# Gates of expert tiles 32 to 127 by adding DMAs into a table in HBM, in place of one-hot products, in a two-layer PEER kernel

## The reference

```python
q = (xt @ w_q).reshape(n_tok, 8, 2, 128)
s = einsum('thpc,hpkc->thpk', q, sub_keys)
sv, si = top_k(s, 16)
cand = sv[:, :, 0, :, None] + sv[:, :, 1, None, :]
cand_idx = si[:, :, 0, :, None] * 128 + si[:, :, 1, None, :]
best, pos = top_k(cand.reshape(n_tok, 8, 256), 16)
eidx = take_along_axis(cand_idx, pos)
g = softmax(best)
act = gelu(einsum('ted,td->te', u_tab[eidx], x))
out = einsum('te,ted->td', g * act, v_tab[eidx])
```

## Time and profile before

| | us |
|---|---|
| median of 3 runs (lowest, highest) | 2098.67 (2096.07, 2100.24) |
| the profiled execution | 2098.75 |
| its span, first to last instruction | 2096.9 |

### The profile page before, as it was taken

How to read it: one execution, slowest core, us unless ns; L and a number is a source line. 1 busy time by engine, 2 the same in 40 slices (tenths; PEclk the granted TensorE clock), 3 DMA queues, 4 the chain that set the end, 5 groups by cost and what they waited for, 6 DMA issues and landing times.

```text
span 2096.9 us, 40394 instructions
## 1 busy us (share of the span) xinstructions
PE 2055.7 (98%) x16458; PEld 1889.3 (90%) x16458; DVE 1635.7 (78%) x3068; ACT 960.7 (46%) x1642; POOL 339.8 (16%) x245
## 2 busy tenths in 40 slices
PE   8999999999999999999999999999999999999998
PEld 7899999999889988887897999999998899888886
DVE  7887995555887688978799779965557777789776
ACT  5654553344433343445655545533334433444443
POOL 0014000000000064642110050000000000456420
PEclk9999999999999999999999999999999999999999
DMA  5354554444554457897322435544445544567873
GB/s 180 111 156 130 178 158 157 154 154 157 171 171 147 145 163 233 293 316 230 125 90 65 145 123 163 170 156 154 148 157 172 171 147 147 163 228 259 301 245 103
DMA packets 112935, 358.34 MB, mean 171 GB/s; under 512 B 17264, under 2 KB 27760, under 8 KB 112496
## 3 DMA queue, kind: packets, MB, share of 16 engines
q1 hardware_dynamic: 99888, 319.99, 47.2%
q0 software_dynamic: 12288, 33.60, 4.9%
q10 hardware_dynamic: 576, 2.18, 0.3%
HBM read 349.09 MB, written 6.63 MB: 170 GB/s over the span
## 4 chain that ended last, share of the span: by engine, by line
PE 84%; DVE 12%; ACT 2%; issue 2%; DMA 1%; SPq 0%; DVEq 0%; ACTq 0%
PE ps L878 15%; PE ps L879 14%; PE ps L880 14%; PE ps L909 11%; PE ps L910 10%; PE ps L911 10%; PE ps L956 6%; DVE w_lo L1470 2%; DVE work L1356 2%; DMA land<-stream_dram 1%; ACT w_hi L583 1%; PE ps L1037 1%; DVE hidden L1356 1%; DVE work L1364 0%; DVE hidden L1376 0%
## 5 line engine op out<-in xcount | busy, mean ns | idle before, releaser
L1470 DVE TENSOR_TENSOR w_lo<-land,w_hi 128x1024 fp32r<-128x1024 f32 x562 | 684.8, 1219 | 275.3 <-ACT w_hi L583 274.7
L583 ACT CAST w_hi<-land 128x1024 fp32r<-128x1024 f32 x592 | 621.2, 1049 | 441.1 <-PE ps L911 351.0
L878 PE MATMUL ps<-act_hi,w_hi 128*128 128x288 f32 x2688 | 809.2, 301 | 12.8 <-DVE act_lo L1196 5.9
L879 PE MATMUL ps<-act_hi,w_lo 128*128 128x288 f32 x2688 | 794.9, 296 | 0.0
L880 PE MATMUL ps<-act_lo,w_hi 128*128 128x288 f32 x2688 | 791.9, 295 | 0.0
L878 PEld LDWEIGHTS ps<-act_hi,w_hi 128*128 128x128 f32 x2688 | 505.4, 188 | 18.4 <-issue 10.9
L880 PEld LDWEIGHTS ps<-act_lo,w_hi 128*128 128x128 f32 x2688 | 507.7, 189 | 0.0
L879 PEld LDWEIGHTS ps<-act_hi,w_lo 128*128 128x128 f32 x2688 | 506.7, 188 | 1.0
L909 PE MATMUL ps<-w_hi,g_hi 128*128 128x512 f32 x1024 | 404.9, 395 | 3.6 <-DVE g_lo L1745 3.6
L910 PE MATMUL ps<-w_lo,g_hi 128*128 128x512 f32 x1024 | 399.1, 390 | 0.0
L911 PE MATMUL ps<-w_hi,g_lo 128*128 128x512 f32 x1024 | 398.8, 389 | 0.0
(11 more groups left out here) (214 smaller groups left out, 1353.8 us busy)
## 6 DMA issues: line engine op xcount, KB each, us to landing
land<-stream_dram SPq DMA_DIRECT2D x592, 512.0 KB
act_d<-smp_stage SPq DMA_DIRECT2D x64, 64.0 KB, 3.3
hidden<-stream_dram,smp_idx POOLq DMA_INDIRECT x128, 5.5
x<-x_dram SPq DMA_DIRECT2D x4, 288.0 KB, 6.8
y_t_dram<-hidden SPq DMA_DIRECT2D x8, 144.0 KB, 1.9
work<-keys_dram SPq DMA_DIRECT2D x1, 1024.0 KB, 7.5
smp_act<-act_d,smp_idx POOLq DMA_INDIRECT x64
work<-keys_dram ACTq DMA_DIRECT2D x1, 1024.0 KB, 9.0
```

The lines of the kernel that those rows point to most:

```text
L583: nc.scalar.copy(w_hi[:, m, :], land[:, n % LANDS, :]).then_inc(w_hi_ready, 1)
L878: nc.tensor.matmul(out, w_hi[:, slot, wsl], hi, start=start, stop=False)
L879: nc.tensor.matmul(out, w_lo[:, slot, wsl], hi, start=False, stop=False)
L1470: V.tensor_tensor(w_lo[:, k, :], land[:, n % LANDS, :], w_hi[:, k, :].bitcast(F32), ALU.subtract).then_inc(lo_by_dve, 1)
```

## The change

One-hot products stay for tiles 0 to 31 (16 chunks per layer). For tiles 32 to 127 there is a table in HBM, `gates_d`, of 128 x 128 x 256 cells (j, i, token), one table per layer.

- *Clearing.* 16 stores of 1 MB per table, issued by ScalarE behind a split: for layer 0 at slabs 3 to 33 of layer 0, from a zeroed stretch of `hidden`; for layer 1 at slabs 142 to 187 of layer 0, from a zeroed stretch of `work`. VectorE waits for the first 16 stores before `first_level` of layer 0.
- *Adding.* Behind `soften`, VectorE makes the cell numbers and the values (`prepare_adds`). GpSimd then issues 256 indirect DMAs that add 128 values each, one per partition (a token), to their cells. They go by head; from the second head on a wait for the adds of the same half of the tokens, of the head before, stands ahead of 16 adds. `fetch_samples` stands behind them on GpSimd.
- *Loading.* 48 times per layer SyncE loads two tiles' gates (256 KB) into one of four buffers, behind the slabs 195, 197, and so on; ahead of the first it waits for all adds. VectorE multiplies two tiles of `hidden` by them (`apply_pair`) at slabs 194, 196, ..., 286.
- *Moved.* The load of the convolution state now waits for all clearing stores, and the load of the keys goes from slab 264 to slab 290.

```diff
-GTOK = (16, 8, 16)
...
+ONE_HOT = BLOCKS[0][1]
+GTOK = 16
+GATES = TP // GTOK
...
+ONEHOTS_AT = [ROUTED + c * (BLOCK_START[0] - 4 - ROUTED) // GATES for c in range(GATES)]
+
+PAIRS = (P - ONE_HOT) // 2
+GATED = GATES + PAIRS
+GATE_LANDS = 4
+APPLY_AT = [min(BLOCK_START[1] - 6 + 2 * k, SLABS - 10 - (PAIRS - 1 - k) * 3 // 2) for k in range(PAIRS)]
+ADDS = PICKS // HEADS
+ZEROS = 16
+ZERO_AT = ([3 + 2 * z for z in range(ZEROS)], [BLOCK_START[0] + 6 + 3 * z for z in range(ZEROS)])
...
+        gates_d = [nc.dram_tensor(f"gates_d{i}", (P, P, TP), F32).ap() for i in range(DEPTH)]
...
+                L, r = divmod(n, SLABS)
+                for k in range(PAIRS):
+                    if r == APPLY_AT[k] + 1:
+                        if k == 0:
+                            for u in range(2):
+                                sp.wait_ge(gate_added[u], 16 * PICKS * (L + 1))
+                        sp.wait_ge(gated, GATED * L + GATES + max(0, k - GATE_LANDS + 1))
+                        two = slice(ONE_HOT + 2 * k, ONE_HOT + 2 * k + 2)
+                        sp.dma_start(gate_land[:, k % GATE_LANDS, :],
+                                     gates_d[L][:, two, :].rearrange("j i t -> j (i t)")
+                                     ).then_inc(gate_landed[k % GATE_LANDS], 16)
...
+            nc.gpsimd.memset(zeros[0], 0.0).then_inc(zeros_ready, 1)
...
+            def add_gates(L):
+
+                pool.wait_ge(adds_ready, L + 1)
+                pool.wait_ge(zeroed, 16 * ZEROS * (L + 1))
+                cells = gates_d[L].rearrange("j i (t one) -> (j i t) one", one=1)
+                for h in range(HEADS):
+                    for u in range(2):
+                        if h:
+                            pool.wait_ge(gate_added[u], 16 * (PICKS * L + ADDS * h))
+                        for k in range(h * ADDS, h * ADDS + ADDS):
+                            nc.gpsimd.indirect_dma_start(
+                                out=cells, out_offset=bass.IndirectOffsetOnAxis(ap=add_idx[:, u, k:k + 1], axis=0),
+                                in_=add_val[:, u, k:k + 1], in_offset=None, compute_op=ALU.add
+                            ).then_inc(gate_added[u], 16)
...
                 if n == POOL_END - 1:
+                    add_gates(0)
                     fetch_samples(0)
                     wide_weights()
                 if n == TOTAL - 1:
+                    add_gates(1)
                     fetch_samples(1)
...
+            def zero(L, r):
+
+                if r in ZERO_AT[L]:
+                    z = ZERO_AT[L].index(r)
+                    act.wait_ge(zeros_ready, L + 1)
+                    rows = gates_d[L].rearrange("j i t -> j (i t)")
+                    act.dma_start(rows[:, z * 2048:z * 2048 + 2048], zeros[L]).then_inc(zeroed, 16)
...
-                        act.wait_ge(gated, GATES * L + GATE0[b] + GCH[b])
+                        act.wait_ge(gated, GATED * L + GATES + max(0, (e - ONE_HOT) // 2 + 1))
...
                     if r == BLOCK_START[2] and L == 0:
+                        act.wait_ge(zeroed, 16 * ZEROS * DEPTH)
+                        act.dma_start(cstate, cstate_d).then_inc(cstate_in, 16)
+                    if r == SLABS - 6 and L == 0:
+                        act.wait_ge(gated, GATED)
                         act.dma_start(keys, keys_d[1]).then_inc(loaded_l, 16)
-                        act.dma_start(cstate, cstate_d).then_inc(loaded_l, 16)
...
+            def prepare_adds(L):
+
+                for u in range(2):
+                    cell = add_val[:, u, :]
+                    did(V.tensor_scalar(cell, picks_tok[:, u, 0, :], float(TP), tok_row[:, u:u + 1],
+                                        ALU.mult, ALU.add))
+                settle()
+                for u in range(2):
+                    cell = add_val[:, u, :]
+                    did(V.scalar_tensor_tensor(out=cell, in0=picks_tok[:, u, 1, :], scalar=float(P * TP), in1=cell,
+                                               op0=ALU.mult, op1=ALU.add))
+                settle()
+                did(V.tensor_copy(add_idx, add_val))
+                settle()
+                V.tensor_copy(add_val, picks_tok[:, :, 2, :]).then_inc(adds_ready, 1)
+
+            def apply_pair(L, k):
+
+                e = ONE_HOT + 2 * k
+                for half in range(2):
+                    dve.wait_ge(evacuated[half], L * USES + USE_U + (e + 2) // 2)
+                count = L * len(range(k % GATE_LANDS, PAIRS, GATE_LANDS)) + k // GATE_LANDS + 1
+                dve.wait_ge(gate_landed[k % GATE_LANDS], 16 * count)
+                at = e % HELD
+                two = hidden[:, at:at + 2, :].rearrange("p i t -> p (i t)")
+                V.tensor_tensor(two, gate_land[:, k % GATE_LANDS, :], two, ALU.mult).then_inc(gated, 1)
...
+                if L == 0:
+                    dve.wait_ge(zeroed, 16 * ZEROS)
                 lo_next, skipped = [base + POOL_END], [0]
...
+                prepare_adds(L)
                 index_samples(L)
...
+                    if r == BLOCK_START[0] and L == 0:
+                        dve.wait_ge(expanded, GATES)
+                        V.memset(zeros[1], 0.0).then_inc(zeros_ready, 1)
+                    while paired < PAIRS and APPLY_AT[paired] <= r:
+                        apply_pair(L, paired)
+                        paired += 1
...
+            row_p = view(work_f, E, P)
+            did(V.tensor_tensor(row_p, ident[:, :], iota[:, :], ALU.mult))
+            settle()
+            did(V.tensor_reduce(tok_row[:, 0:1], row_p, AX_X, ALU.add))
+            settle()
+            did(V.tensor_scalar(tok_row[:, 1:2], tok_row[:, 0:1], float(P), None, ALU.add))
```

More of the change, by code:

```diff
@@ L386, in build @@
         gated = sem("gated")
+        zeros_ready = sem("zeros_ready")
+        zeroed = sem("zeroed")
+        adds_ready = sem("adds_ready")
+        gate_added = [sem("gate_added_0"), sem("gate_added_1")]
+        gate_landed = [sem(f"gate_landed_{k}") for k in range(GATE_LANDS)]
+        cstate_in = sem("cstate_in")
         g_hi_ready = sem("g_hi_ready")
@@ L637, in layer @@
                         split(base + IN0 + n + LEAD)
+                        zero(0, IN0 + n)
                         if n == 0:
@@ L728, in layer @@
                     split(base + OUT0 + n + LEAD)
+                    if L == 0:
+                        zero(0, OUT0 + n)
                     if n:
@@ L747, in layer @@
                     split(base + Q0 + n + LEAD)
+                    if L == 0:
+                        zero(0, Q0 + n)
                     if n == 0:
@@ L791, in layer @@
                     split(base + r + LEAD)
+                    if L == 0:
+                        zero(1, r)
                     if r == SLABS - 5 and L == 0:
@@ L944, in turn_back, with expand @@
                     mm.then_inc(y_turned, 1)
-            def expand(L, b, c):
-                g = GATES * L + GATE0[b] + c
+            def expand(L, c):
+                g = GATES * L + c
                 pe.wait_ge(onehots_ready, g + 1)
[L949 to L954, removed]
+                if c >= 2:
+                    pe.wait_ge(gated, GATED * L + c - 1)
+                j, mask, terms = onehot_views(g % 2)
+                n = ONE_HOT
+                for t in range(GTOK):
                     for k in range(TERMS):
@@ L1141, in layer @@
                     while chunk < GATES and ONEHOTS_AT[chunk] + 1 <= r:
-                        b = max(k for k in range(len(BLOCKS)) if GATE0[k] <= chunk)
-                        expand(L, b, chunk - GATE0[b])
+                        expand(L, chunk)
                         chunk += 1
@@ L1580, in soften, with onehots @@
                                 ALU.mult).then_inc(picks_ready, 1)
[L1582 to L1587, removed]
+            def onehots(L, c):
+                g = GATES * L + c
+                j, mask, terms = onehot_views(g % 2)
+                tok = slice(c * GTOK, (c + 1) * GTOK)
+                if c >= 2 or L:
                     dve.wait_ge(expanded, g - 1)
-                for out, keys_of, kind, n in ((mask, iota_rep[:, lo:hi, :], 0, hi - lo), (j, iota_rep, 1, KEYS)):
-                    shape = [P, GTOK[b] // 2, n, 2]
+                for out, keys_of, kind, n in ((mask, iota_rep[:, 0:ONE_HOT, :], 0, ONE_HOT), (j, iota_rep, 1, KEYS)):
+                    shape = [P, GTOK // 2, n, 2]
                     did(V.tensor_tensor(out, keys_of.unsqueeze(1).to_broadcast(shape),
@@ L1737, in peer @@
                     while applied < GATES and ONEHOTS_AT[applied] + 2 <= r:
-                        b = max(k for k in range(len(BLOCKS)) if GATE0[k] <= applied)
-                        apply(L, b, applied - GATE0[b])
+                        apply(L, applied)
                         applied += 1
+                    if r == BLOCK_START[0] and L == 0:
[4 more added lines that the diff above has]
+                        paired += 1
                     if r + 1 in VISITS:
@@ L1749, in peer @@
```

(7 more changed lines are left out.)

48 lines of the change are left out of this document (17 added, 31 removed).

## The result

The changed kernel takes 2304.3 us (median of 4 executions, 2299.17 to 2307.53) where the kernel before, on the same chip, took 2098.72: a ratio of 1.098 [1.0955, 1.1002]. It is slower by 206 us, outside the range, on the side of the second rival and dearer than its 2193. The profiled execution took 2305.2 us with a span of 2303.4.

A forecast was written before the change was run, and what follows sets the result against it. TensorE was taken as the bound, with adds on GpSimd hidden at zero cost: 2098.75 - 94.7 (products) + 6.5 (clearing) + 3.4 (routing) + 0.9 (start) + 8.7 (bandwidth) = 2024 us; own range 2008 to 2060, whole range 2008 to 2200.

The forecast's parts named there:

- the second rival: Adds at 1.82 us on GpSimd come late, SyncE and TensorE wait at slab 195: 2193 us, slower; chance 35%.
- the price of an add: GpSimd's time from one add to the next in the 256 a layer: 1.41 us, bounds 1.25 and 2.35.
- The first term: GpSimd's unhindered time for one add, taken from a gather of 128 single values: 0.94 us.
- VectorE's share: Time that a half-busy VectorE adds to each of GpSimd's adds: 0.17 us.
- break-even: Add price on GpSimd at which the 38 us net gain of a layer is used up: 1.64 us.
- the cushion: Slack before adds delay TensorE near slab 196: 0.08 us each, 1.49 us allowed against 1.41 forecast.
- The rule: If GpSimd's time followed two read descriptors per chunk, an add would take 2.35 us and the kernel 2464 us.
- The gross gain: One-hot product chunks removed from TensorE's path, 0.83 and 1.30 us each: 94.7 us in two layers.
- The clearing's wait: VectorE in layer 0 waits for 16 clearing stores, delaying matmuls near slab 48: 6.5 us once, bounds 0 and 16.
- Routing: Six VectorE instructions preparing cells and values, on the path: 1.7 us a layer, 3.4 in two, bounds 1 to 4.
- Bandwidth: Table loads beside the stream in slabs 226 to 284: 4.4 us a layer, 8.7 in all, bounds 0 and 29 a layer.
- Waits from head to head: GpSimd's waits for 16 adds issued 16 adds earlier, over 20 us ago: hidden, no cost.

The follow-up runs named there:

- e2: The changed kernel with its 256 indirect DMAs a layer storing their values in place of adding them; 2044.16 us (one execution).
- e3: The changed kernel with 64 cells in place of 128 for each of the 256 adds a layer; 2218.31 us (one execution).
- e7: e1 with the adds' cell numbers and values worked out later, at slab 84 behind two chunks of one-hots; 2007.65 us (one execution).
- e1: The changed kernel with half of the adds (heads 0 to 3, 128 of 256 a layer); 2017.91 us, ratio 0.9615.

## Why the prediction was wrong

**The step that failed** is the price of an add, "0.94 + 0.30 + 0.17 = 1.41 us". The first term was a gather's and stood for an add; an add alone takes 1.55 us. The 0.30 between two is 0.30 in the trace, and VectorE's share, forecast at 0.17, came out at 0.20 for the adds (1.75 less 1.55) and 0.26 for the stores of e2 (1.21 on average, less 0.95). Together an add took 2.05 beside working engines, against a break-even that the prediction itself put at 1.64. The first term made the loss, but the cushion was gone without it: the stores of e2, nearly at a gather's price, came 1.56 us apart where 1.49 was allowed, and late. The bounds for the first term, 0.94 and 1.88, held the truth; I took the lower end because bytes didn't count in the gathers, and that reason bore on bytes, not on the kind of operation. With a cushion of 0.08 us and an unknown of up to 0.94, the likeliest case should have been the late one.

**The second rival** had the mechanism and the place: SyncE at slab 195, the stream and TensorE behind it. Its reason, two things to read, is at most half of it by e3. Its price, 1.82 us, was too low by 0.19 to 0.26 (2.01 and 2.08 apart over a whole layer), which over 256 adds and two layers is some 115 us, about the difference between its 2193 and 2304.

**The rule** that a reduce in the DMA engines reads two sources for each chunk (the Trainium skill, "Collectives: The Full Stack", section "The bandwidth ceiling") pointed the right way. Taken as twice GpSimd's time it gave 2.35 us an add and 2464 us in all; the trace has 1.55 alone and about 2.05 in place, and by e3 at most half of the extra time goes with the number of cells.

**The gross gain**, 94.7 us, held: slabs 200 to 226, which lost 9 chunks, went from 82.7 to 70.8 us (1.32 a chunk, forecast 1.30), and slabs 136 to 190, which lost 27, from 179.9 to 158.3 (0.80, forecast 0.83).

**The clearing's wait** was 1.9 us where I had 6.5. The last store was issued at 157.53 us, 1.2 later than predicted, but VectorE went on at 162.41, 4.9 us later and not 8.2. Its wait:

```profile
DVE hidden L1524 <- DMA gates_d<-hidden: 13.1, 1, 13.1
```

**Routing** was mis-sized the other way: 3.4 and 4.1 us a layer, where I had 1.7 (six instructions) within bounds of 1 to 4 for both layers together. The six instructions themselves took 1.66 us in layer 0 (308.16 to 309.82); the rest is what e7 leaves open.

**Bandwidth** in slabs 226 to 284: 58 slabs of 2.72 us are 157.8; the changed kernel took 164.2 and 159.8. In layer 0, 3.2 of the 6.4 us lost were there before (slabs 256 to 284 took 79.4 against 76.2), so some 3 and 2 us came in, where I had 4.4 a layer. Waits from head to head cost nothing, as said: GpSimd's longest pause between two adds in its waits is 1.5 us.

```profile
POOL gates_d L527 <- issue: 157.4, 510, 1.5
```

So the sum but for one term was within 4 us of the truth, and that term was 285 us. Some of that closeness is luck: the clearing's wait was forecast 4.6 us too dear and bandwidth some 4, and routing 4 too cheap.

## What to carry to other kernels

A train of small DMAs is priced by what the issuing engine spends on each, times their number, against the one time by which all must be done; work that time out first, then ask how far the price can move before it passes. A price borrowed from a neighbouring operation (a gather for an add) must carry its whole uncertainty into the choice of the likeliest case, and if the cushion is smaller than that, the late case is the forecast. Where the dear part is an option of the operation (here the addition), see whether an engine with idle time can do that part, and lay that work in small pieces where nothing behind it is due.

## What the runs showed of the hardware

- An indirect DMA of 128 single values kept GpSimd 0.95 us as a store (e2) and 1.55 us as an add; an add of 64 values 1.40 us (e3). Between two of them lay 0.30 us as a rule.
- The same add took 1.55 us while it met no VectorE instruction, whether TensorE worked or stood still, and 1.80 us on average (up to 2.51) where it met one beside a busy TensorE (layer 0 of the changed kernel). A store went from 0.96 us without to 1.29 on average with one (layer 0 of e2).
- In the stall TensorE was idle and the granted clock read 0.52 from 700 to 824 us, near the 1.2 GHz level. Slab 195, the first behind it, still ran at that level: its matmuls began 0.24 us apart in place of 0.13, and it took 5.64 us where it takes 3.20 in e1. From slab 196 on the clock was 1.00. So each stand of TensorE was followed by a loss of some 2 us more (5.64 and 5.22 against 3.20). The two stretches (columns as in the earlier trace rows):

```profile
832.00:837.60 5.60, 5.57 (x24) 5.60 (x25) 3.20 (x4) 2.46 (x4) 0.00 (x0) 0.52 0.84 293
837.70:842.00 4.30, 4.30 (x35) 4.30 (x34) 2.35 (x3) 2.35 (x6) 0.00 (x0) 1.00 0.90 293
```

- A cleared megabyte, stored from one stretch of memory to rows far apart, landed in 5.9 us (layer 0) and 6.4 us (layer 1) in the median beside the stream of slabs; the last one of layer 0 took 4.9.
